# Laying out a bias band and a row of norms by GpSimd copies and DMAs through DRAM in place of TensorE, in a fused encoder layer

## What is computed

```python
u = rms_norm(h, g_pre_mix)                    # norms over the 1024 channels of each token
proj = jnp.einsum('bsd,de->bse', u, w_in)     # 1024 -> 2304 columns
...
def relative_bias_band(rel_bias):             # (32 buckets, 4 heads) -> (4, 64, 128)
    qi = jnp.arange(64)[:, None]
    kj = jnp.arange(128)[None, :]
    rel = kj - 64 - qi
    return jnp.transpose(rel_bias[t5_bucket(rel)], (2, 0, 1))
...
s = jnp.einsum('bcqhgd,bckhd->bhgcqk', qc, kb) * scale + bias_band   # chunk window attention
```

## Time and profile before

| | |
|---|---|
| median of 3 runs | 1008.52 us (1008.32 to 1010.45) |
| the profiled execution: span | 1008.5 us |
| PE busy | 997.8 us (99%) |
| DVE busy | 779.9 us (77%) |
| ACT busy | 575.6 us (57%) |
| POOL busy | 77.5 us (8%) |
| HBM read, written | 65.46 MB, 8.39 MB |

### The profile page before, as it was taken

How to read it: one execution, slowest core, us unless ns; L and a number is a source line. 1 busy time by engine, 2 the same in 40 slices (tenths; PEclk the granted TensorE clock), 3 DMA queues, 4 the chain that set the end, 5 groups by cost and what they waited for, 6 DMA issues and landing times.

```text
span 1008.5 us, 12248 instructions
## 1 busy us (share of the span) xinstructions
PE 997.8 (99%) x4884; PEld 811.0 (80%) x4884; DVE 779.9 (77%) x727; ACT 575.6 (57%) x752; POOL 77.5 (8%) x66
## 2 busy tenths in 40 slices
PE   9999999999999999999999999999999999999997
PEld 7878778897777787888888888888888888888885
DVE  6237759898796689878777778887777887777998
ACT  7424643777886457768544656433657333647346
POOL 0014213001222230000000000000000000000000
PEclk9999999999999999999999999999999999999999
DMA  9511111200101743031031031031031031035004
GB/s 346 172 42 43 42 42 42 65 21 1 43 1 43 272 164 108 1 128 40 1 126 41 1 125 43 1 125 42 1 125 42 1 125 42 1 125 209 1 1 166
DMA packets 38352, 74.64 MB, mean 74 GB/s; under 512 B 3444, under 2 KB 11928, under 8 KB 38296
## 3 DMA queue, kind: packets, MB, share of 16 engines
q1 hardware_dynamic: 38152, 73.83, 21.2%
q10 hardware_dynamic: 144, 0.03, 0.0%
HBM read 65.46 MB, written 8.39 MB: 73 GB/s over the span
## 4 chain that ended last, share of the span: by engine, by line
PE 91%; DVE 5%; ACT 2%; issue 1%; DMA 0%; POOL 0%; DVEq 0%; SPq 0%; ACTq 0%
PE ps L769 27%; PE ps L771 27%; PE ps L773 27%; PE ps L783 2%; PE ps L952 2%; PE ps L1001 2%; PE ps L1026 2%; PE ps L867 1%; PE ps L1099 1%; DVE m_row L1984 0%; DVE out_gained L2276 0%; DVE work L1982 0%; PE ps L982 0%; DVE y L2361 0%; ACT work L1366 0%
## 5 line engine op out<-in xcount | busy, mean ns | idle before, releaser
L769 PE MATMUL ps<-a_op,b_op 128*128 128x512 f32 x448 | 175.4, 391 | 0.6 <-DVE a_op L2150 0.6
L773 PE MATMUL ps<-a_op,b_op 128*128 128x512 f32 x448 | 174.4, 389 | 0.0
L771 PE MATMUL ps<-a_op,b_op 128*128 128x512 f32 x448 | 174.3, 389 | 0.0
L769 PE MATMUL ps<-b_op,a_op 128*128 128x512 f32 x448 | 174.3, 389 | 0.0
L771 PE MATMUL ps<-b_op,a_op 128*128 128x512 f32 x448 | 174.3, 389 | 0.0
L773 PE MATMUL ps<-b_op,a_op 128*128 128x512 f32 x448 | 174.3, 389 | 0.0
L1584 ACT CAST a_op<-f 128x1024 fp32r<-128x1024 f32 x56 | 58.8, 1050 | 112.1 <-PE ps L773 82.3
L2161 DVE TENSOR_TENSOR b_op<-wq,b_op 128x1024 fp32r<-128x1024 f32 x96 | 117.0, 1218 | 0.0
L2150 DVE TENSOR_TENSOR a_op<-f,a_op 128x1024 fp32r<-128x1024 f32 x56 | 68.5, 1223 | 50.0 <-ACT a_op L1584 50.0
L1592 ACT CAST b_op<-wq 128x1024 fp32r<-128x1024 f32 x96 | 100.7, 1049 | 0.1
L769 PEld LDWEIGHTS ps<-a_op,b_op 128*128 128x128 f32 x448 | 84.1, 188 | 18.2 <-DVE a_op L2150 1.1
(11 more groups left out here) (235 smaller groups left out, 1733.4 us busy)
## 6 DMA issues: line engine op xcount, KB each, us to landing
wq<-in_w_ff_in SPq DMA_DIRECT2D x16, 1024.0 KB, 5.5
wq<-in_w_ff_out SPq DMA_DIRECT2D x16, 1024.0 KB, 5.1
stage<-in_w_in SPq DMA_DIRECT2D x16, 512.0 KB, 4.6
y<-in_x SPq DMA_DIRECT2D x4, 1024.0 KB, 13.6
h_spill<-y SPq DMA_DIRECT2D x8, 512.0 KB, 2.7
h_back<-h_spill SPq DMA_DIRECT2D x2, 2048.0 KB, 12.1
out<-y SPq DMA_DIRECT2D x8, 512.0 KB, 2.7
stage<-in_w_out SPq DMA_DIRECT2D x6, 512.0 KB, 3.3
```

The lines of the kernel that those rows point to most:

```text
L769: nc.tensor.matmul(dst, stat[0], mov[0], start=first, stop=False, skip_group_check=chained)
L771: nc.tensor.matmul(dst, stat[0], mov[1], start=False, stop=False, skip_group_check=chained)
L773: return nc.tensor.matmul(dst, stat[1], mov[0], start=False, stop=last, skip_group_check=chained)
```

## The change

- The bias row: the bias table is loaded turned (4 heads by 32 buckets), and POOL writes each head's row of 191 values by 29 copies, one for each run of equal buckets. SP stores the row 64 times for each head (256 rows of 191 values at a pitch of 192), waits, and reads it back by two DMAs with a pitch of 191, which makes each row one element earlier than the last: that is the band as it is used, on 128 partitions. No matmul and no copy by ACT is left of it.
- The row of norms: SP waits for `rstd`, stores its 1024 values one by one to DRAM in the order of the tokens, waits, and loads them as one row to 128 partitions.
- The waits of PE, ACT and DVE for the steps that are gone are taken out; ACT's first squares now wait for the first half of g = 0 (their scratch is also PE's warm-up operand).

```diff
-            sp.dma_start(onehot_c, onehot).then_inc(rel_loaded, 16)
-            sp.dma_start(rel_c[0:REL_BUCKETS, :], rel_bias).then_inc(rel_loaded, 16)
+            sp.dma_start(rel_c[0:4, :], rel_by_head).then_inc(rel_loaded, 16)
...
-            sp.wait_ge(rel_copied, 1)
-            sp.dma_start(rel_dram, rel_row).then_inc(rel_stored, 16)
+            sp.wait_ge(rel_spread, 1)
+            sp.dma_start(rel_dram[:, :, 0:REL_SPAN], rel_row[0:4, 0:REL_SPAN].unsqueeze(1)
+                         .to_broadcast([4, CHUNK, REL_SPAN])).then_inc(rel_stored, 16)
             sp.wait_ge(rel_stored, 16)
-            sliding = bass.AP(rel_dram.tensor, 0, [[1, CHUNK], [REL_SPAN + 1, 4], [1, P]])
-            sp.dma_start(rel_slide, sliding).then_inc(rel_back, 16)
+            head = CHUNK * (REL_SPAN + 1)
+            for a in range(2):
+                sliding = bass.AP(rel_dram.tensor, head * a + CHUNK - 1,
+                                  [[REL_SPAN, CHUNK], [2 * head, 2], [1, P]])
+                sp.dma_start(bias_band[HEAD * a:HEAD * (a + 1), :]
+                             .rearrange("p (v k) -> p v k", v=2), sliding).then_inc(band_loaded, 16)
...
             load_in(2, w_in[0], IN_COLS[2])
+            sp.wait_ge(rstd_ready, 1)
+            sp.dma_start(rs_dram.rearrange("(i p) -> p i", p=P), rstd[:, 0:TOK],
+                         allow_slow_non_contiguous=True).then_inc(rs_stored, 16)
+            sp.wait_ge(rs_stored, 16)
+            sp.dma_start(rs_row[:, :], rs_dram.partition_broadcast(P)).then_inc(rs_row_ready, 16)
...
-            after(nc.gpsimd.memset(flip, 0.0))
-            nc.gpsimd.affine_select(out=flip...
+            pool.wait_ge(rel_loaded, 16)
+            for first, width, bucket in bucket_runs():
+                ins = nc.gpsimd.tensor_copy(rel_row[0:4, first:first + width],
+                                            rel_c[0:4, bucket:bucket + 1].to_broadcast([4, width]))
+            ins.then_inc(rel_spread, 1)
...
-                if half == 0:
-                    pe.wait_ge(rel_loaded, 32)
-                    nc.tensor.matmul(ps[0:4, 4, 0:REL_SPAN + 1], rel_c[0:REL_BUCKETS, :], onehot_c,
-                                     start=True, stop=True).then_inc(rel_summed, 1)
...
-                        if f == 4:
-                            pe.wait_ge(rel_copied, 1)
-                        elif f == 6:
-                            pe.wait_ge(rs_row_ready, 1)
-                        elif f >= 8:
+                        if f >= 8:
...
-                        elif f == 5:
-                            feature_major(g, n, half, {2: spread_norms})
...
-                        if f == 8:
-                            pe.wait_ge(proj_copied, 8)
-                            pe.wait_ge(rel_back, 16)
-                            nc.tensor.matmul(ps[:, 5, :], flip, work[0:CHUNK, 2, 0:4 * P],
-                                             start=True, stop=True).then_inc(band_ready, 1)
...
-            act.wait_ge(rel_summed, 1)
-            nc.scalar.copy(rel_row, ps[0:4, 4, 0:REL_SPAN + 1]).then_inc(rel_copied, 1)
...
+            act.wait_ge(proj_ready, 2)
...
-            spread_copy()
...
-            dve.wait_ge(rs_row_ready, 1)
+            dve.wait_ge(rs_row_ready, 16)
```

More of the change, by code:

```diff
@@ L9 @@
+import itertools
 import math
@@ L76, with bucket_runs, encoder_layer @@
 REL_SPAN = 3 * CHUNK - 1
-def bucket_onehot():
+def bucket_runs():
     starts = [0, 1, 2, 3, 4, 5, 6, 7, 8, 12, 16, 23, 32, 46, 64, 91]
[L82 to L91, removed]
+    half = REL_BUCKETS // 2
+    buckets = [sum(abs(m - (2 * CHUNK - 1)) >= s for s in starts) - 1
+               + (half if m > 2 * CHUNK - 1 else 0) for m in range(REL_SPAN)]
+    runs = []
+    for b, ms in itertools.groupby(range(REL_SPAN), key=lambda m: buckets[m]):
+        ms = list(ms)
+        runs.append((ms[0], len(ms), b))
+    return runs
+def encoder_layer(nc, x, w_in, lru_wa, lru_wx, swa_sinks, w_out, g_post_mix, w_ff_in,
+                  w_ff_out, g_post_mlp, rel_by_head, x_turned, columns, w_first, out):
     h_dram = nc.dram_tensor("h_spill", [S, D], F32, kind="Internal").ap()
-    rel_dram = nc.dram_tensor("rel_row", [4, REL_SPAN + 1], F32, kind="Internal").ap()
+    rel_dram = nc.dram_tensor("rel_rows", [4, CHUNK, REL_SPAN + 1], F32, kind="Internal").ap()
+    rs_dram = nc.dram_tensor("rs_tokens", [S], F32, kind="Internal").ap()
     with ExitStack() as ctx:
@@ L183, in encoder_layer @@
         sink_c = const("sink_c", 2)
-        rel_c = const("rel_c", 4)
+        rel_c = const("rel_c", REL_BUCKETS)
+        rel_row = const("rel_row", REL_SPAN + 1)
         eps_c = const("eps_c", 1)
@@ L200, in encoder_layer @@
         gate_w = work[:, 5, 0:LRU_TILES * P].rearrange("p (c f) -> p c f", c=LRU_TILES)
[L201 to L204, removed]
         ps = ctx.enter_context(nc.psum_tensor("ps", [P, 8, BANK], F32))
@@ L226, in encoder_layer @@
         warm_ready = sem("warm_ready")
-        tables_ready, flip_ready = sem("tables_ready"), sem("flip_ready")
+        tables_ready = sem("tables_ready")
         ident_ready = sem("ident_ready")
         gate_w_loaded = sem("gate_w_loaded")
-        rel_summed, rel_copied, rel_stored, rel_back = (
-            sem("rel_summed"), sem("rel_copied"), sem("rel_stored"), sem("rel_back"))
-        band_ready, band_copied = sem("band_ready"), sem("band_copied")
+        rel_spread, rel_stored, band_loaded = (
+            sem("rel_spread"), sem("rel_stored"), sem("band_loaded"))
         lam_abs, lam_ln, lam_done = sem("lam_abs"), sem("lam_ln"), sem("lam_done")
@@ L235, in encoder_layer @@
             sem("sumsq_ready"), sem("rs0_ready"), sem("rstd_ready"))
-        rs_spread, rs_row_ready, eps_ready = (
-            sem("rs_spread"), sem("rs_row_ready"), sem("eps_ready"))
+        rs_stored, rs_row_ready, eps_ready = (
+            sem("rs_stored"), sem("rs_row_ready"), sem("eps_ready"))
         xt_ready, u_hi_ready, u_lo_ready = (
@@ L826, in token_values @@
                 mm.then_inc(proj_ready, 1)
[L828 to L835, removed]
             def token_major(slot, a_hi, a_lo, s, ks, bank, first=0, last=OUT_K - 1):
@@ L1233, in first_rsqrt @@
                     .then_inc(rs0_ready, 1)
-            def spread_copy():
-                act.wait_ge(rs_spread, 1)
-                for half in range(2):
-                    ins = nc.scalar.copy(rs_row[:, BANK * half:BANK * (half + 1)],
-                                         ps[:, 5 + 2 * half, :])
-                ins.then_inc(rs_row_ready, 1)
             def group_rsqrt(grp):
@@ L1303, in recurrent @@
                 if c == 0:
-                    act.wait_ge(band_copied, 2)
                     act.wait_ge(lam_done, 1)
@@ L1329, in _ @@
             for g in range(N_IN):
-                if g == 2:
-                    act.wait_ge(band_ready, 1)
-                    by_head = ps[:, 5, :].rearrange("p (v a k) -> p v a k", v=2, a=2)
-                    for a in range(2):
-                        rows = slice(HEAD * a, HEAD * (a + 1))
-                        nc.scalar.copy(bias_band[rows, :].rearrange("p (v k) -> p v k", v=2),
-                                       by_head[rows, :, a, :]).then_inc(band_copied, 1)
                 for c in range(LRU_TILES):
@@ L1862, in convolution @@
                 dve.wait_ge(proj_copied, tile_copied(c // 2, c % 2))
-                if c == 0:
-                    dve.wait_ge(band_copied, 2)
-                else:
+                if c:
                     dve.wait_ge(lru_done, c)
@@ L1974, in window_max @@
                 if h == 0:
-                    dve.wait_ge(band_copied, 2)
+                    dve.wait_ge(band_loaded, 32)
                 first = int(h < 2)
@@ L2412, in _ @@
             final(7)
-INPUTS = ["x", "w_in", "lru_wa", "lru_wx", "swa_sinks", "rel_bias", "w_out", "g_post_mix", "w_ff_in",
+INPUTS = ["x", "w_in", "lru_wa", "lru_wx", "swa_sinks", "w_out", "g_post_mix", "w_ff_in",
           "w_ff_out", "g_post_mlp"]
@@ L2428, in laid_out @@
     by_partition = [in_tiles(name) for name in COLUMNS]
-    return {"onehot": bucket_onehot(),
+    return {"rel_by_head": np.ascontiguousarray(np.asarray(inputs["rel_bias"]).T),
             "x_turned": np.ascontiguousarray(np.asarray(inputs["x"])[0].reshape(2, BANK, KD, P)
```

2 lines of the change are left out of this document (removed).

## The result

The changed kernel takes 1020.08 us (median of 4 runs, 1019.6 to 1020.12), the kernel before 1008.52. The ratio is 1.0107, with a 95% interval of 1.0095 to 1.0119. So the change makes the kernel slower, by 1.1%. The forecast was 1008.0 us, and the measured time lies 6.9 us beyond 1013.2, the upper end that the prediction gave. The profiled execution has a span of 1018.4 us against 1008.5.

The account below looks back on a forecast made before the run. PE was taken to bound the kernel, busy 997.8 of 1008.5 us. Removing 2.76 us from PE and adding a 2.2 us wait at f = 8 gave -0.55, so 1008.0 us; range 1005.7 to 1013.2.

Parts of the forecast that it names:

- first rival: Slower: norms' single-element stores are dear and everything behind waits; 1013.1 us at 100 ns each, 1017 at the end; chance 0.30.
- step 1: SP's store of the bias rows, 196 KB: 2.2 us plus 0.75 to the release, so released at 32.85.
- step 4: Store of 1024 norms behind g = 2's weights: 20 ns each, 1.3 us, plus 0.75 to the release, at 44.05.
- What comes off PE: Three PE interruptions removed, two band matmuls and the norms' spread: 0.62, 0.88 and 1.26 us, together 2.76 us.
- POOL's copies: 29 copies for the bias row, 0.29 us each, 8.4 us at most; hidden behind x's bytes, costed at nothing.
- middle case: Dear norm elements at 100 ns, between the two ends: 6.4 us instead of 1.3, result 1013.1 us.
- Steps 2, 3, 5 and 6: SP's issues done at 38.0, g = 2's weights by 42.0, row's load 4.7 us, DVE's copies and rests 4.75 us.
- The gates: PE reaches the gates at 69.8 with their inputs ready at 67.4: 2.4 us of cover, costed at nothing.

Follow-up runs that it names:

- short_norms: late_band with the sinks' loads left in front of g = 2's weights and the norms turned by one PE transpose, stored as 8 rows of 512 B; 1006.14 us, ratio 0.9973.
- one_copy: The changed kernel with one POOL copy in place of the 29 for the bias row; one run, 1022.5 us.
- band_only: The changed kernel with the norms spread by TensorE as before, so only the band goes through DRAM; 1007.01 us, ratio 0.998.
- padded_store: The changed kernel with the 1024 norms stored 64 B apart and the row loaded from another tensor; one run, 1014.53 us.
- norms_only: The kernel before with only the norms sent through DRAM, the band by TensorE as before; 1015.04 us, ratio 1.0055.
- half_store: The changed kernel storing only 512 of the norms, side by side, with the row loaded from another tensor; one run, 1020.25 us.
- late_band: The changed kernel with SP's order altered: g = 2's weights behind x, then the norms, band DMAs and sinks behind g = 4's weights; 1013.42 us, ratio 1.0043.
- wide_store: The changed kernel with the norms stored as 128 pieces of 32 B instead of 1024 of 4 B; 1012.83 us, ratio 1.0035.

## Why the prediction was wrong

It named the right chain, the right place of the wait and, in its first rival, the right step. Two terms of the sum were too small and one was not in it, all to the same side. With what was measured the sum closes: 1008.0 + 3.4 (step 1) + 4.1 (step 4) + 2.8 (the clock) = 1018.3, and the span is 1018.4; the median is another 1.7 us above, which is the distance of time and span.

- **What comes off PE (2.76 us): right.** The pauses at 18.6, 37.6 and 58.3 are gone, and short_norms, which waits neither at f = 8 nor at the gates, is 2.76 us under the kernel before (1.7 to 3.8 by the interval); that the two figures agree to a hundredth is chance, since 0.1 us was spent again on the transpose. That POOL's copies and the band's way are hidden was right as well (one_copy, band_only), although a copy is 0.40 us and not 0.29 at most.
- **Step 4, the store of the norms (2.05 us behind the weights): wrong, and the step on which it fell.** It took 6.2 us behind the 4 of the weights ahead. Both the forecast and the rival with the dear elements sought the price in the packets, one element after the other. These cost 10 ns, at the lower bound; the price is behind them, in the 5.9 us between the last packet and the release, and it is no price for each element, since half of them cost the same. The 0.75 us for the release came from the store of the bias row, 3 KB in four rows of 768 B; it was carried over to a store of which it says nothing. The rival did name that all write at once into 4 KB of DRAM, and its middle case (6.4 us and 0.75 for the release) was near the 6.2 in size, though not in its reason. The time came out beyond even its end, 1017, because the rows' store and the clock came on top. The rule cited there (below 512 B an engine reads, modifies and writes) is in "DMA: Bandwidth & Descriptors" of the Trainium skill, section "Specifications". padded_store writes elements as small and is released 1.1 us behind its last packet, so the rule alone does not give this price; that writes so close together make it dear is what the runs add.
- **Step 1, the store of the rows (released at 32.85): mis-sized.** Released at 36.21. I gave a quarter of the engines a quarter of the full rate, 89 GB/s. Measured are 26 GB/s, since an engine takes 0.1 us for a packet of 764 B; at the full rate a packet carries 3.7 KB in 163 ns. The rule of the Trainium skill that the prediction cites, in "DMA: Bandwidth & Descriptors", section "Why a DMA increments its semaphore by 16 and not by 1", gives four engines for this store, and the 3.3 busy engines seen here agree with it; what was missing was the price of a packet on each of them. The error is 3.4 us, and the release lies beyond even the upper bound of 4.4 for this term, which would give 35.05. What sets the 0.1 us stays open.
- **Steps 2, 3, 5 and 6: right.** SP's issues from 36.2 to 41.3, the weights of g = 2 flowed by some 45 us (4 us after their last issue), the row landed in 4.6 us (forecast 4.7), DVE's stretch 56.26 to 61.01 (4.75).
- **A term that was not there: the clock.** A wait of 11 us costs its length and 2.84 us of matmuls at 1.2 GHz behind it. The forecast had a wait of 2.2 us and no such term, and the rivals with longer waits had none either.
- **The gates:** forecast with cover left, and PE does not wait there.
- **What I read wrongly of the time before.** I wrote that the span lies within 0.1 us of the median. In every run of all these kernels the time is 1.7 to 1.8 us longer than the span. So the profiled execution of before must have been one of some 1010.2 us, and not a median one: its first matmuls ran at half the pace until 9.8 us (0.85 us for a pair, 0.46 in the change's profile), some 1.6 us more. band_only fits this: its first matmuls ran at half pace only until some 7 us, and its gates begin at 67.02 instead of 70.48, 3.5 us earlier, of which the matmuls for the band are 1.9. Of 16 runs of the kernel before beside band_only, ten took 1008.3 to 1008.9 us and six 1009.4 to 1010.6, which agrees with two such starts. So the medians differ by 11.6 us and the two spans by only 9.9: against an execution of before with a quick start the change is 11.5 us longer, and it keeps nothing of its own quick start, since f = 8 begins when a chain of DMAs ends. Not all of this is clear: the profile of norms_only has the slow start too, and its execution took 1016.03 us, 0.9 to 1.1 us more than its other three, although f = 8 hangs on the DMAs there as well.

In sum, the wait at f = 8: forecast 2.2; + 3.4 (step 1) + 4.1 (step 4: 51.5 instead of 44.05, less those 3.4) makes 9.7, + 1.6 for PE's quicker start makes the 11.3 seen.

## What to carry to other kernels

Price a DMA that something waits for by its issue-to-release time, not by its bytes or packets: a store of many neighbouring small values can have sent its packets within 1.5 us and be reported done 6 us later. Turn such data into a few long rows first (8 rows of 512 B took 1.24 us in all), even at the price of a small matmul. And where a change makes PE wait some microseconds in the middle of its work, add to the wait the matmuls at the lower clock behind it.

Two edits that are harmless or even good alone can be costly together if they share a queue: the band's wait on SP was free until the norms' store stood behind it.

## What the runs showed of the hardware

- Release of a store after its last packet: 5.9 to 7.5 us for single values side by side (the change 5.9, half_store 6.0, norms_only 6.5, late_band 7.5), 1.1 us at a pitch of 64 B, 0.6 for pieces of 32 B (wide_store), 0.3 for rows of 512 B (short_norms).
- 256 rows of 764 B from four partitions: 3.3 of 16 engines busy, 26 GB/s, 0.1 us for a packet.
- PE's granted clock fell to 0.50 in every wait at f = 8 in this study, or at its end, of which the shortest was 3.66 us (wide_store) and the longest 13.4 (one_copy). The matmuls behind cost 1.5 us more in late_band (f = 8 to the gates 17.97 us instead of 17.70 - 1.26 = 16.44), 2.5 in wide_store, 2.6 in norms_only and 2.8 in the change. No shorter wait was tried, so what the forecast 2.2 us would have done is not known.
- The first matmuls can run at half pace while the granted clock reads 1.00. PE's timeline of the kernel before, then of the change, each row a pair of matmuls (0.85 us and 0.46 us from pair to pair), and for each the window of that stretch:

```profile
7.28 1.05 PE L783 MATMUL ps<-act_lo,w_hi 128*128 128x512 f32 x2
8.13 1.05 PE L783 MATMUL ps<-act_hi,w_hi 128*128 128x512 f32 x2
...
5.50:9.80 4.30, 4.30 (x10) 3.38 (x11) 3.24 (x6) 2.90 (x6) 0.00 (x0) 1.00 1.04 398
```

```profile
6.31 0.62 PE L790 MATMUL ps<-act_lo,w_hi 128*128 128x512 f32 x2
6.76 0.62 PE L790 MATMUL ps<-act_hi,w_hi 128*128 128x512 f32 x2
...
5.50:9.80 4.30, 3.91 (x17) 2.88 (x17) 2.86 (x5) 2.73 (x5) 0.00 (x0) 1.00 1.02 383
```

There are 10 matmuls against 17 in the same 4.3 us, so there the distance between matmuls tells the pace, and the clock's column does not. What sets it in a given execution, no run here shows.
